# Inverting the chunk matrices of a gated-delta scan with 64-wide blocks from the first level on

## The reference, cut to what matters

```python
a_mat = jnp.where(strict, jnp.einsum('nbhid,nbhjd->nbhij', kb, kc) * decay, 0.0)
t_mat = lax.linalg.triangular_solve(eye + a_mat, eye, left_side=True, lower=True, unit_diagonal=True)
u = jnp.einsum('nbhij,nbhjd->nbhid', t_mat, vc * bc[..., None])
w = jnp.einsum('nbhij,nbhjd->nbhid', t_mat, kb * jnp.exp(g)[..., None])
def step(s, inp):
    v_new = uc - jnp.einsum('bhcd,bhde->bhce', wc, s)
    o = jnp.einsum('bhcd,bhde->bhce', qd, s) + jnp.einsum('bhij,bhje->bhie', qkc, v_new)
    s = s * gl[..., None, None] + jnp.einsum('bhcd,bhce->bhde', kd, v_new)
```

## Time and profile before

| | us |
|---|---|
| median of 3 runs (lowest, highest) | 4019.65 (4015.51, 4023.67) |
| the profiled execution's own time | 4023.99 |
| its span, first to last instruction | 4022.3 |
| PE busy in the span | 3074.6 |
| DVE, ACT, POOL busy | 1169.9, 703.6, 408.0 |
| mean granted PE clock | 0.859 |

### The profile page before, as it was taken

The page is one execution under the profiler, slowest core; times in us unless marked ns, Lnnn a source line. Parts: engine busy times, 40 slices in busy tenths (PEclk is TensorE's granted clock), DMA queues, the critical chain, the costliest instruction groups (busy, mean ns, idle before and its releaser), DMA issues. The chain is left out here.

```text
span 4022.3 us, 61945 instructions
## 1 busy us (share of the span) xinstructions
PE 3074.6 (76%) x22574; PEld 1609.2 (40%) x22575; DVE 1169.9 (29%) x2165; ACT 703.6 (17%) x1630; POOL 408.0 (10%) x407
## 2 busy tenths in 40 slices
PE   4999996666664974899998828757789739978992
PEld 1455443556663334333333213335554423323330
DVE  3322331344446125011110161125552240100114
ACT  2211211111112011000000031126662100000002
POOL 0000001122221110000000031111111100000002
PEclk8999998666666985999999959879999759989996
DMA  5311101222203543777988350031112238987883
GB/s 203 118 40 45 52 17 33 97 65 66 66 24 127 210 154 143 291 294 318 388 363 337 145 205 26 28 115 39 38 38 95 106 131 365 376 334 327 327 342 155
DMA packets 152728, 668.16 MB, mean 166 GB/s; under 512 B 25888, under 2 KB 61888, under 8 KB 121824
## 3 DMA queue, kind: packets, MB, share of 16 engines
q1 hardware_dynamic: 123456, 540.33, 34.6%
q0 software_dynamic: 19504, 72.03, 4.7%
q10 hardware_dynamic: 9584, 53.19, 3.2%
HBM read 596.12 MB, written 69.39 MB: 165 GB/s over the span
## 5 line engine op out<-in xcount | busy, mean ns | idle before, releaser
L1650 PE MATMUL bank<-w,xT 128*64 x3392 | 752.3, 602 | 52.1 <-DMA w<-in_moe_w 41.6
L536 PE MATMUL bank<-aT,w 128*128 128x512 f32 (+1 forms) x1344 | 498.7, 534 | 8.0 <-DVE short L704 5.9
L1650 PEld LDWEIGHTS bank<-w,xT 128*64 128x64 f32 x3392 | 242.0, 139 | 523.0 <-issue 517.3
L1670 PE MATMUL bank<-w,hT 128*64 (+1 forms) x1696 | 381.3, 603 | 38.2 <-issue 38.1
L536 PEld LDWEIGHTS bank<-aT,w 128*128 128x128 f32 x1344 | 264.6, 198 | 237.9 <-issue 222.1
L1742 DVE TENSOR_TENSOR h<-h,bank 128x512 f32<-128x512 f32 x53 | 36.5, 688 | 782.9 <-PE bank L1650 782.9
L1670 PEld LDWEIGHTS bank<-w,hT 128*64 128x64 f32 x1696 | 122.3, 138 | 296.1 <-issue 296.1
L1940 PE MATMUL bank<-at_w_in,aT 128*128 128x512 f32 x416 | 191.4, 622 | 3.0 <-PEq L117 3.0
L2129 PE MATMUL bank<-eye,probs 128*128 128x128 f32 x640 | 102.2, 292 | 42.7 <-ACT probsT L2192 42.5
L1626 PE MATMUL bank<-eye,x 128*128 128x128 f32 x440 | 65.6, 295 | 82.4 <-DMA x<-moe_x,idx_block 58.3
L1940 PEld LDWEIGHTS bank<-at_w_in,aT 128*128 128x128 f32 x416 | 83.1, 202 | 105.7 <-issue 105.7
(11 more groups left out here) (335 smaller groups left out, 4135.7 us busy)
## 6 DMA issues: line engine op xcount, KB each, us to landing
w<-in_moe_w SPq DMA_DIRECT2D x180, 2048.0 KB, 14.2
ada_w<-in_ada_w SPq DMA_DIRECT2D x48, 1024.0 KB, 11.4
moe_y<-y ACTq DMA_DIRECT2D x53, 512.0 KB
w<-in_moe_w ACTq DMA_DIRECT2D x12, 2048.0 KB, 12.2
w<-in_ab_w_in SPq DMA_DIRECT2D x28, 512.0 KB, 4.7
moe_x<-w SPq DMA_DIRECT2D x18, 512.0 KB, 2.6
moe_y<-zero POOLq DMA_DIRECT2D x1, 8192.0 KB, 26.5
at_w_in<-in_at_w_in SPq DMA_DIRECT2D x3, 2048.0 KB
```

Source lines behind the costliest of these rows:

```text
L536: mm = pe.matmul(k.bank[3 * s + n][:, 0:width], w[j][:, c, :], aT[:, c, at:at + width], start=(c == 0), stop=(c == KC - 1))
L1650: mm = pe.matmul(k.bank[UP[half]][u * UNIT:(u + 1) * UNIT, :], xT[:, c, u * UNIT:(u + 1) * UNIT], w13[:, r if u else ds(buf[0], 1), half, ...
L1670: mm = pe.matmul(k.bank[Y[half]][u * UNIT:(u + 1) * UNIT, :], hT[:, c, u * UNIT:(u + 1) * UNIT], w2[:, r if u else ds(buf[0], 1), at:at + ...
```

## The change

`SUB` goes from 32 to 64 and `SUB_LEVELS` from 5 to 6. The compact form now keeps the two 64 x 64 blocks on the diagonal, X is 128 x 512 values per direction and `Pm` 128 x 256. There are five compact levels (blocks of 4 to 64) with 64 x 64 matmuls on the two diagonal tiles of the array, and one last merge to 128. The merge to 64 on 32 x 32 tiles is gone, with `Tf`, `P5`, their copies on ACT and DVE, and one of three counts of `tf_ready`. The constant masks grow, since they follow `SUB`.

```diff
-SUB, SUB_LEVELS = 32, 5
-NSUB = P // SUB
+SUB, SUB_LEVELS = 64, 6
...
-    MERGES, XS, TFS = IN_SUB + 2, IN_SUB + 1, 3
+    MERGES, XS = IN_SUB + 1, IN_SUB + 1
...
-                for b in range(0, P // 2, SUB):
-                    r = d * (P // 2) + b
-                    nc.scalar.copy(Tf[d][at(r), :, at(b)], T_sub(d)[at(r)])
-            for d in R2:
-                act.wait_ge(u_ready[d], primed(s * MERGES + MERGES - 1))
-                lo, hi = low_high(d, d)
-                nc.scalar.activation(Tf[d][at(hi), :, at(lo - d * P // 2)], sub[d][2][at(hi)], ACT.Copy,
-                                     scale=-1.0).then_inc(tf_ready[d], 1)
-                for p in R2:
-                    lo, hi = low_high(p, d)
-                    c = nc.scalar.activation(TT[d][at(lo), :, at(hi)], sub[d][3][at(lo)], ACT.Copy, scale=-1.0)
-                c.then_inc(tf_ready[d], 1)
             for d in R2:
                 act.wait_ge(u_ready[d], primed(s * MERGES + MERGES))
-                lo, hi = low_high(0, d, P // 2)
-                nc.scalar.activation(TT[d][at(lo, P // 2), :, at(hi, P // 2)], halves[d][3][at(lo, P // 2)], ACT.Copy,
-                                     scale=-1.0).then_inc(tf_ready[d], 1)
+                lo, hi = low_high(d)
+                nc.scalar.activation(TT[d][at(lo), :, at(hi)], sub[d][3][at(lo)], ACT.Copy, scale=-1.0).then_inc(tf_ready[d], 1)
...
-                dve.wait_ge(p_ready[d], primed(s * MERGES + MERGES - 1))
-                nc.vector.tensor_copy(Pm[d][:], sub[d][1]).then_inc(pm_ready[d], 1)
-            for d in R2:
                 dve.wait_ge(p_ready[d], primed(s * MERGES + MERGES))
-                _, hi = low_high(0, d, P // 2)
-                nc.vector.tensor_copy(P5[d][at(hi, P // 2)], halves[d][1][at(hi, P // 2)]).then_inc(pm_ready[d], 1)
+                _, hi = low_high(d)
+                nc.vector.tensor_copy(Pm[d][at(hi)], sub[d][1][at(hi)]).then_inc(pm_ready[d], 1)
...
             for d in R2:
+                lo, hi = low_high(d)
                 pe.wait_ge(x_ready[d], primed(s * XS + XS))
                 pe.sem_inc(tiles_begun, 1)
                 for h in range(NH):
-                    for p in R2:
-                        lo, hi = low_high(p, d)
-                        mm = pe.matmul(sub[d][1][at(hi), h, :], AT[d][at(lo), h, at(hi)], T_sub(d)[at(lo), h, :],
-                                       start=True, stop=True)
+                    mm = pe.matmul(sub[d][1][at(hi), h, :], AT[d][at(lo), h, at(hi)], T_sub(d)[at(lo), h, :],
+                                   start=True, stop=True)
                 mm.then_inc(p_ready[d], 1)
...
+                lo, hi = low_high(d)
+                pe.wait_ge(pm_ready[d], primed(s * MERGES + MERGES))
...
+                    mm = pe.matmul(sub[d][3][at(lo), h, :], Pm[d][at(hi), h, :], TT_sub(d)[at(hi), h, :],
+                                   start=True, stop=True)
                 mm.then_inc(u_ready[d], 1)
...
-                pe.wait_ge(tf_ready[d], primed((s + 1) * TFS))
+                pe.wait_ge(tf_ready[d], primed(s + 1))
```

More of the change, by code:

```diff
@@ L746, in delta_scan @@
     X, Pm = [k.sb(f"T_TT_sub{d}", [P, 2, NH, SUB]) for d in R2], [k.sb(f"A_T_off{d}", [P, NH, SUB]) for d in R2]
-    Tf, TT = [k.sb(f"T_half{d}", [P, NH, P // 2]) for d in R2], per_dir("TT")
-    P5 = [k.sb(f"A_T_half{d}", [P, NH, P // 2]) for d in R2]
+    TT = per_dir("TT")
     VB, R, VN, S = per_dir("V_beta"), per_dir("R"), per_dir("v_new"), per_dir("S")
@@ L773, in delta_scan @@
     sub = [[flat[d][n][:, 0:NH * SUB].rearrange("p (h n) -> p h n", h=NH) for n in range(4)] for d in R2]
-    halves = [[flat[d][n][:, 0:NH * P // 2].rearrange("p (h n) -> p h n", h=NH) for n in range(4)] for d in R2]
     def T_sub(d):
@@ L780, in TT_sub, with at, low_high @@
         return X[d][:, 1 - d]
[L782 to L788, removed]
+    def at(b):
+        return slice(b, b + SUB)
+    def low_high(d):
+        return SUB * d, SUB * (1 - d)
     block = k.block()
@@ L852, in _ @@
             nc.gpsimd.memset(TT[d][:], 0.0).then_inc(state_set, 1)
-            nc.gpsimd.memset(Tf[d][:], 0.0).then_inc(state_set, 1)
         pool.wait_ge(stats, primed(1))
@@ L950, in _ @@
         dve.sem_inc(stats, 1)
-        dve.wait_ge(state_set, primed(7))
+        dve.wait_ge(state_set, primed(5))
         st = Steps(dve, order, 2 * (1 + 1 + 1 + 1))
@@ L1028, in _ @@
         pe.wait_ge(stats, primed(1))
-        pe.wait_ge(state_set, primed(7))
+        pe.wait_ge(state_set, primed(5))
         def heads(to, lhs, rhs, start=True, stop=True):
@@ L1090, in body @@
             for d in R2:
-                pe.wait_ge(pm_ready[d], primed(s * MERGES + MERGES - 1))
-                _, hi = low_high(d, d)
+                lo, hi = low_high(d)
+                pe.wait_ge(pm_ready[d], primed(s * MERGES + MERGES))
                 pe.sem_inc(tiles_begun, 1)
                 for h in range(NH):
[L1095 to L1117, removed]
+                    mm = pe.matmul(sub[d][3][at(lo), h, :], Pm[d][at(hi), h, :], TT_sub(d)[at(hi), h, :],
+                                   start=True, stop=True)
```

## The result

The changed kernel takes 3927.3 us (median of 4 runs, 3921.4 to 3930.2) against 4018.4 us: ratio 0.977, 95% interval 0.9753 to 0.9787. The forecast was 3935, in a range of 3885 to 4012. The two profiled executions lie at the far ends of their kernels' runs, so their spans differ by more, 4022.3 - 3919.7 = 102.6 us, than the medians, 91 us. Of these 102.6 the profile puts 99.8 up to the end of the scan: the last rescaling of the state on POOL begins at 1138.0 instead of 1237.8 us. A pass takes 43.6 us on average instead of 53.2; the first pass alone gained 12.9, the other nine 9.6 each.

What follows compares the result with a forecast made beforehand. The prediction took PE in the scan's levels to be bound by instruction supply, not the matrices. Saving 8.5 us a pass, 85 us over ten, gave 3939 from 4024.0, or 3935 on the median; range 3885 to 4012.

Steps and rivals of the forecast that it cites:

- Stalls as lack of instructions: PE in the compact levels: 11.5 us a pass of issue waits come from instruction supply; 1 us a pass left.
- Two tiles side by side, and the clock: Levels: two diagonal 64 x 64 tiles start a record each 0.054 us at half clock, 0.028 at full; full clock returns.
- the rival of the half clock: Levels: the clock stays at half, nothing gained or lost, 4010 to 4030 us; chance 0.11.
- The clock at the start of a pass: Odd passes: full clock may last into the levels, saving 1.9 us more, half of it counted, 0.95.
- The chain of a level: Dependency chain between PE and DVE in one level at full clock: 3.4 us, with PE's 2.7 us inside it.
- Making X: DVE at the start of the levels: 128 x 512 taken at 1.4 us, X ready 1 to 1.5 us later.
- The sum: A regular pass: all terms together save a mean of 8.5 us; ten passes 85 us.
- the half-clock chain: Dependency chain of one level at half clock: 4.8 us, below PE's work of 5.2 us.
- Tiles not side by side: Rival, levels: the two tiles run one after the other, +26.5 us a pass, about 4285 us; chance 0.05.
- Stalls of another kind: Rival, levels: the stalls are not instruction supply and stay at 11.5 us a pass, some 4040 us; chance 0.06.
- the loop's jump: Loop over the passes: its own jump stays after the change; no size or chance given.

Runs made afterwards that it cites:

- The one-tile run: The changed kernel with its five levels worked out for the upper 64 rows alone, half of each level's matmuls left out: 4033.0 us.
- the doses of records: The changed kernel with 24, then 12, more tiny matmuls behind each p group of the levels: 4065.1 and 3982.0 us.
- the runs with other counts: The changed kernel with 24 or 12 tiny matmuls added per p group, 4065.1 and 3982.0 us; the kernel before without each level's second product, 3971.3 us.
- two sensible edits: The changed kernel with the subtraction from X split, 3937.4 and 3937.8 us; or with 128-wide matmuls filling PE's waits before turning, 3923.8 and 3931.5 us.

## Why the prediction was right

- **Stalls as lack of instructions: right.** They went from 115.4 to 1.7 us; I had left 1 us a pass, that is 10. More records bring them back, and fewer records in the kernel before take part of them away.
- **Two tiles side by side, and the clock: right.** 0.85 us a group at half clock (0.86 worked out), 0.47 at full (0.45). In the pass shown the levels are at 1.00 but for the first. The one-tile run shows that both hang on the second tile. It also puts a price on the rival of the half clock: levels of 5.36 us with hardly a stall (1.3 us in the scan) give 4033, just above the rival's 4010 to 4030, so 64-wide matmuls that stayed at half clock would have gained nothing by the stalls that went. With 32-wide ones, fewer stalls alone did gain, 4.5 us a pass.
- **The clock at the start of a pass: the pattern was wrong.** I had counted half of the odd passes with a level 0 at full clock. In the profile it was so in passes 1, 8 and 9 of ten: there DVE's second subtraction from X, of d = 1, starts 3.5 to 3.7 us after the last making of X, elsewhere 4.5 to 5.6. In the second profile of the same kernel it was so in pass 1 alone.
- **The chain of a level: right.** 3.42 us against 3.4.
- **Making X: too dear.** L960 at 128 x 512 takes 0.72 us and not 1.4. Counted from the start of AT of d = 1 (931.52 here, 983.49 in the pass that I had worked on), X of d = 0 is ready at 934.17, 0.7 us earlier than my terms give.
- **The sum: somewhat low.** 8.5 us a pass worked out, 9.6 measured between passes. L960 has 0.7 of the difference of 1.1 and the stalls 0.8, which is 0.4 too much; what gave that back isn't taken apart. I had also taken the first pass as the others, and it gained 12.9. In the profiled executions the scan then gains 99.8 us by the first profile of the changed kernel and 93.6 by the second (last rescaling at 1144.2), against 85; in medians the kernel gains 91. Two small slips change nothing: the half-clock chain adds up to 4.6 and not 4.8 us, and 4012 takes in a tenth of the half-clock case's range and not a quarter.
- **Rivals.** Tiles not side by side: excluded by the 0.85 us. Stalls of another kind: excluded by the doses of records, and the loop's jump by the stalls of the unrolled pass. The rule that different row tiles cannot access the same PSUM bank at once (Trainium skill, "TensorEngine Tiling (Array Packing)", Restrictions and Gotchas) is not borne out: both tiles write one bank, with records 0.053 us apart that last over 0.2 us each. Nor is "mostly hidden" for crossing an instruction block (Trainium skill, "Runtime: NRT & Kernel Launch", Instruction fetch mechanics) in the kernel before, where records come every 0.013 us and 115.4 us of stalls show; in the changed kernel, with 1.7 us, it is.

## What to carry to other kernels

Where PE waits for "issue" in the middle of a group, count its records per packet of the instruction queue before counting array time. Here 128 matmul records with their weight loads came in 3.8 us on average (192 in a level of 5.6 us before the change) and in 4.0 to 4.3 in the runs with other counts, so small matmuls cost instructions, not columns. Larger tiles that keep all 128 rows busy pay twice, since they need fewer instructions and bring back the full clock. And once one bound is gone, look how near the next is: here the chain (3.4 us), PE's work (2.8) and the packets (2.8 to 3.2) lie so close that two sensible edits took only 3 to 12 us off the scan. Compare the stage that was edited as well as the whole: the stages behind the scan moved by up to 30 us with their code unchanged, and hid these gains and a third of another.

## What the runs showed of the hardware that I had not expected

- PE busy in 20.16 of 20.20 us with 64-row matmuls on one tile stays at 1.2 GHz for the whole stretch.
- Matmuls on one tile of the array start among the last ones of the preceding group on another tile; swapping the loops costs 0.68 us a level and not 2.
- The subtraction from the broadcast identity takes 0.72 us (median) with 128 x 512 elements in rows of 64, and took 0.72 with 128 x 256 in rows of 32. No run tells why.
- 48 records with 4 moving columns take 0.57 us, about 0.01 us for a record.
- The stages behind the scan run the same code in all these kernels and took 2781.6 to 2812.0 us. No run tells why.
